# Memory heads over half jobs, late modulation panels outside the ring, half of the second layer's modulation sums in the first mixer

## The chip, the cores and the metric

One core of one Trainium2 chip runs the whole program. The metric is the device time of one execution in microseconds (us), as the median of several runs. Engine names: PE is the TensorE matmul, PEld its weight load, DVE VectorE, ACT ScalarE, POOL GpSimd, SP SyncE (here it only starts transfers).

## What is computed

Three blocks follow each other on 256 tokens of width 1024, all in float32. The first holds a mixer with three branches and a mixture of 16 experts; the second block has two layers, each with a mixer and a feed-forward part (dense in layer 0, eight experts in layer 1).

```python
# first block
proj = x @ w_in            # da_q da_k da_v r_q r_k r_v r_g m_q gates
y_da  = diff_attention(...)      # 8 heads
y_ret = silu(r_g) * retention(...)   # 4 heads
y_mem = memory_attention(m_q, mem @ w_mem_kv)   # 4 heads: softmax(q k) v
merged = sum_n sigmoid(gate_n) * (branch_n @ w_branch[n])
x = layer_norm(ALPHA * x + merged @ w_o); x = layer_norm(ALPHA * x + moe(x))
# second block
cond = silu(c)
for l in range(2):
    mod = cond @ ada_w[l] + ada_b[l]        # 6 vectors of 1024: shift, scale, gain
    h = x * (1 + sc_m) + sh_m; x = layer_norm(ALPHA * x + (1 + g_m) * mixer_l(h))
    h = x * (1 + sc_f) + sh_f; x = layer_norm(ALPHA * x + (1 + g_f) * ff_l(h))
```

## The kernel before, in words

**Precise products.** A float32 weight is used as two numbers: ACT writes a rounded copy ("hi"), DVE subtracts it from the weight and writes the rest ("lo"), and PE adds three products (hi with hi, hi with lo, lo with hi). In the mixers one such piece is 128x1024, called a chunk. A job (`gemm`) is two chunks of 24 matmuls of 256 columns; a "turned" job pair (`da_v`, `r_v`, `m_v`) is four chunks of 12 matmuls of 512 columns. hi copies stand in four places in turn (`HI_HOMES`), so ACT can't copy chunk n+4 before PE has used chunk n; the lo overwrites the panel in its slot.

**Order.** `mixer1_steps` writes the order of the first mixer out by hand. All engines walk the same list, each doing its part of a step, with semaphores between them. A `stage` step (hi and lo of a whole job) is put by `with_stages` ahead of the job before. In the eight first heads the steps are finer: `HEAD_FILL` gives each head two jobs, cut into four chunks (`part` for PE, `hi` for ACT, `lo` for DVE), laid between score, turn and out of the head. Two of the lo's (`now[2]`, `now[3]`) are made by DVE inside the two scores. The memory heads of the first mixer are coarser: a score, a whole `gate2` job, the turn of the head before, a whole `branch1` job, the out.

**Panels.** Weights come as panels of 2 MB, two jobs in each, on SP's queue, in the order of the plan. In the first mixer they go round four slots (`plan_loads`); a load waits until the panel that had the slot is done with, and SP stands still for it, so each later load waits as well.

**Modulation.** `mod` needs 24 panels of 2 MB of `ada_w_2` (12 per layer), each of which DVE multiplies with `cond_row` and sums, in four instructions (`sum_modulation`, L1408). Layer 0's twelve, steps `("ada", 0, n)`, go through the same four slots in the first mixer. Layer 1's twelve are taken in the dense feed-forward part: `half_loads` (L984) starts 24 loads of 1 MB from POOL into two places, and `sum_half` (L1418) makes one sum behind each of the 48 chunks 6 to 53 of 70. Load j may start when half j-2 has been summed.

**Feed-forward.** `unit` runs 70 chunks of the dense part: G, U (12 matmuls of 512 columns), turn, D. There are six places for chunks (`STAGES`) and three slots for panels. The lo of a chunk is L1764, the hi L1290; PE waits for the lo. SP starts the panel after next when DVE has made the four lo's of the slot's panel. For each pair DVE makes h (L1896) from ACT's silu (L1344), and PE may begin the next G only then where nothing else is in between.

**Table loads.** ACT's functions come in sets; `keep_ln_exp` loads the set with exp ahead of time. Sigmoid needs another set.

## Time and profile before

| | |
|---|---|
| median of 3 runs | 2211.27 us (2209.21 to 2212.22) |
| the profiled execution | 2206.13 us, its span 2204.3 us |
| first mixer, start to last of its matmuls | 0 to 485 us |
| dense feed-forward part | 886 to 1092 us |
| PE busy | 2101.5 us, 95% |
| DVE, ACT busy | 1750.0 us (79%), 1403.2 us (64%) |
| granted clock of TensorE, mean | 0.98 of full |

The profiled execution lies 5 us below the median, and its span 1.8 us below its own time. A row of the trace gives start, duration, engine, line, operation and, in square brackets, how long the engine stood idle before it and what ended that. A table of waits gives the sum, how many and the longest.

### The profile page before, as it was taken

To read this page: it belongs to the slowest core of one execution; us is meant where nothing else is said; L and a number is where in the kernel's file an instruction comes from. 1 tells how busy PE (TensorE), PEld (TensorE's weight loads), DVE (VectorE), ACT (ScalarE), POOL (GpSimd) and SP (SyncE) were. 2 spreads that over 40 slices of the span, in tenths; PEclk is the share of its full clock that TensorE was granted. 3 is DMA by queue.
4 is the path that set the end of the run, shared out by engine and by line. 5 is a ranking of instruction groups with operands and counts; after the bars stand their busy time and mean duration, and the time that the engine had idled before them with its cause. 6 is when DMAs were issued, how large, how long until landed. Compare 5 with 4: busy or idle time off the path is not lost.

```text
span 2204.3 us, 27381 instructions
## 1 busy us (share of the span) xinstructions
PE 2101.5 (95%) x10956; PEld 1788.4 (81%) x10956; DVE 1750.0 (79%) x2099; ACT 1403.2 (64%) x1707; POOL 42.7 (2%) x54
## 2 busy tenths in 40 slices
PE   8999999989999987899988999999999999999997
PEld 7888898888888876677878888888888888888886
DVE  2676677669988865767565899999999999999897
ACT  3566344547777654433353777887778778877774
POOL 0000000000000000000000000000000000000000
PEclk9999999989999999899998999999999999999999
DMA  8543676739999950678632799999999999999994
GB/s 313 210 153 115 252 300 254 282 125 376 385 372 375 376 196 1 256 297 311 235 160 115 287 392 368 389 365 390 361 388 362 393 377 375 379 367 378 386 395 152
DMA packets 59806, 659.26 MB, mean 299 GB/s; under 512 B 6288, under 2 KB 12304, under 8 KB 19088
## 3 DMA queue, kind: packets, MB, share of 16 engines
q1 hardware_dynamic: 49104, 608.32, 70.9%
q0 software_dynamic: 7152, 38.80, 4.4%
q10 hardware_dynamic: 3408, 10.22, 1.2%
q8 instruction: 92, 1.51, 0.3%
q14 instruction: 50, 0.41, 0.1%
HBM read 645.79 MB, written 11.53 MB: 298 GB/s over the span
## 4 chain that ended last, share of the span: by engine, by line
PE 77%; DVE 11%; DMA 7%; ACT 3%; issue 2%; ACTq 0%; DVEq 0%; SPq 0%
PE psum L2270 52%; PE psum L2012 11%; PE psum L1990 4%; DVE stage_lo L1764 3%; DMA arena<-ada_w_in 3%; PE psum L2059 3%; PE psum L1965 1%; PE psum L2405 1%; DMA ring<-moe_w_gate_in 1%; DVE arena L1418 1%; DVE ring L1408 1%; PE psum L2049 1%; DVE arena L767 1%; DMA ring<-moe_w_up_in 1%; DVE mixer_split L1532 1%
## 5 line engine op out<-in xcount | busy, mean ns | idle before, releaser
L1764 DVE TENSOR_TENSOR stage_lo<-ring,stage_hi 128x1024 fp32r<-128x1024 f32 (+1 forms) x934 | 1099.4, 1217 | 85.0 <-ACT stage_hi L1290 72.2
L1290 ACT ACTIVATE stage_hi<-ring 128x1024 fp32r<-128x1024 f32 (+1 forms) x934 | 953.4, 1053 | 281.3 <-PE psum L2270 151.8
L2270 PE MATMUL psum<-stage_hi,x_hi 128*128 128x512 f32 (+1 forms) x1344 | 531.6, 396 | 13.6 <-DVE arena L1896 10.1
L2270 PE MATMUL psum<-stage_hi,x_lo 128*128 128x512 f32 (+1 forms) x1344 | 522.2, 389 | 0.0
L2270 PE MATMUL psum<-stage_lo,x_hi 128*128 128x512 f32 (+1 forms) x1344 | 520.9, 388 | 0.0
L2270 PEld LDWEIGHTS psum<-stage_hi,x_hi 128*128 128x128 f32 x1344 | 253.4, 189 | 66.1 <-issue 10.3
L2270 PEld LDWEIGHTS psum<-stage_hi,x_lo 128*128 128x128 f32 x1344 | 252.9, 188 | 53.6
L2270 PEld LDWEIGHTS psum<-stage_lo,x_hi 128*128 128x128 f32 x1344 | 253.7, 189 | 49.0
L2270 PE MATMUL psum<-stage_hi,h_hi 128*128 128x512 f32 x664 | 261.9, 394 | 7.9 <-DVE stage_lo L1764 4.4
L2012 PE MATMUL psum<-mixer_split 128*128 128x256 f32 x1280 | 252.3, 286 | 13.4 <-DVE ring_split L1532 4.9
L2270 PE MATMUL psum<-stage_lo,h_hi 128*128 128x512 f32 x664 | 259.4, 391 | 0.0
L2012 PEld LDWEIGHTS psum<-mixer_split 128*128 128x128 f32 x1280 | 199.8, 193 | 16.7 <-issue 12.6
L2270 PE MATMUL psum<-stage_hi,h_lo 128*128 128x512 f32 x664 | 205.1, 390 | 0.0
L2012 PE MATMUL psum<-arena_split,mixer_split 128*128 128x256 f32 x928 | 187.8, 286 | 2.6 <-DVE mixer_split L1532 1.9
L1532 DVE TENSOR_TENSOR ring_split<-ring,mixer_split 128x1024 fp32r<-128x1024 f32 x98 | 116.2, 1220 | 63.0 <-ACT mixer_split L1042 62.9
L2270 PEld LDWEIGHTS psum<-stage_hi,h_hi 128*128 128x128 f32 x664 | 124.9, 188 | 36.0 <-DVE h_lo L1908 5.6
L2012 PEld LDWEIGHTS psum<-arena_split,mixer_split 128*128 128x128 f32 x928 | 145.4, 189 | 6.3 <-issue 5.8
L2270 PEld LDWEIGHTS psum<-stage_hi,h_lo 128*128 128x128 f32 x664 | 125.1, 188 | 26.5
L2270 PEld LDWEIGHTS psum<-stage_lo,h_hi 128*128 128x128 f32 x664 | 125.1, 188 | 25.1
L1042 ACT ACTIVATE mixer_split<-ring 128x1024 fp32r<-128x1024 f32 x98 | 99.3, 1053 | 46.3 <-DMA ring<-w_mem_kv_in 14.2
L1351 ACT ACTIVATE h_hi<-psum 128x512 fp32r<-128x512 f32 (+1 forms) x84 | 48.1, 580 | 84.4 <-PE psum L2405 84.4
L2012 PE MATMUL psum<-mixer_split,ring_split 128*128 128x256 f32 x304 | 85.4, 281 | 0.0
(266 smaller groups left out, 1971.6 us busy)
## 6 DMA issues: line engine op xcount, KB each, us to landing
ring<-moe_w_gate_in SPq DMA_DIRECT2D x56, 2048.0 KB, 9.7
ring<-moe_w_up_in SPq DMA_DIRECT2D x56, 2048.0 KB, 9.8
ring<-moe_w_down_in SPq DMA_DIRECT2D x56, 2048.0 KB, 10.0
ring<-w_in SPq DMA_DIRECT2D x48, 2048.0 KB, 10.1
ring<-w_in_in SPq DMA_DIRECT2D x12, 2048.0 KB, 8.6
arena<-ada_w_in POOLq DMA_DIRECT2D x24, 1024.0 KB, 7.7
ring<-ada_w_in SPq DMA_DIRECT2D x10, 2048.0 KB, 9.3
mixer_tiles<-w_in_in SPq DMA_DIRECT2D x7, 2048.0 KB, 8.5
```

The costliest lines, as they stand in the source:

```text
L767: settle(dve.bn_stats(bn_s[:, t, 6 * half:6 * half + 6], bank(b)))
L1042: act.activation(staged_hi(q, n), staged_source(q, c, False), ACT.Copy).then_inc(w_hi_set, 1)
L1290: act.activation(chunk_view(stage_hi, f, side, p, c), chunk_source(f, side, p, c), ACT.Copy)\
L1351: ins = act.activation(h_hi[:, 0:blocks, h_columns(f, p, t)], bank(t0 + t, 4, P)[:, 0:blocks, :], ACT.Copy)
L1408: ins = dve.tensor_tensor_reduce(wt[:, m, :], wt[:, m, :], cond_row, 1.0, 0.0, ALU.mult, ALU.add, mod[:, c:c + 1])
L1418: ins = dve.tensor_tensor_reduce(wt, wt, cond_row, 1.0, 0.0, ALU.mult, ALU.add, mod[:, c:c + 1])
L1532: dve.tensor_tensor(staged_source(q, c, True), staged_source(q, c, False), staged_hi(q, n).bitcast(F32), ALU.subtract).then_inc(w_lo_set, 1)
L1764: dve.tensor_tensor(chunk_view(stage_lo, f, side, p, c), chunk_source(f, side, p, c), chunk_view(stage_hi, f, side, p, c).bitcast(F32), AL ...
L1990: ins = pe.matmul(bank(banks[t]), xt[:, 2 * c + k, tokens], wt[:, k, :], start=(c + k + m == 0), stop=(c == 3 and k == 1 and m == 2))
L2012: ins = pe.matmul(bank(b, 2, T)[:, m, :], wt[:, k, :], xt[:, k, :], start=(k + j == 0), stop=(k == KT - 1 and j == 2))
L2059: ins = pe.matmul(bank(b, 2, T)[:, m, :], wt[:, k, c:c + P], rhs[:, k, :], start=(k == 0), stop=(k == KT - 1))
L2270: ins = pe.matmul(dst, a, b, start=start, stop=stop)
```

## The change

`ADA_MIXER1` = 18 panels are now summed in the first mixer: twelve of layer 0 and six of layer 1. Panels 0 to 10 go through the four slots. Panels 11 to 17 have a place of their own, `ada_late`, one panel in size, over the retention's q, k and v; POOL loads it (`late_loads`, ahead of its other work): the first when the last `ret_out` is done, each further one when the one before has been summed. Panels 3 to 6 are summed in halves, two instructions in each of the eight first heads; panels 0 to 2 lie between `da_k` and `da_v` jobs.

Each memory head now takes four chunks, `branch1` h and `gate2` h (`MEM_CHUNKS`), between score, turn and out, as the first heads do; the lo of `now[2]` is made inside the score. `keep_ln_exp` follows every sigmoid of gate 2 and the last of gate 1.

In the dense feed-forward part twelve loads of 1 MB and 24 sums stay; the first sum is at chunk 12, and then one at every second chunk.

```diff
@@ -49,6 +49,7 @@
...
 LAMBDA_INIT = 0.2
+ADA_MIXER1, ADA_LATE = 18, 11
...
@@ -121,6 +122,7 @@
...
+MEM_CHUNKS = [[((name, h), c) for name in ("branch1", "gate2") for c in range(2)] for h in range(MEM_H)]
...
@@ -173,8 +175,8 @@
...
-    s = gemms("da_q", 0) + splits("x", 0, 1, 2, 3) + gemms("da_q", 1, 2, 3) + gemms("da_k", 0, 1, 2, 3)
-    s += gemms("da_v", 0, 1) + ada(0) + [(side, *HEAD_CHUNKS[0][c]) for side in ("hi", "lo") for c in range(2)]
+    s = gemms("da_q", 0) + splits("x", 0, 1, 2, 3) + gemms("da_q", 1, 2, 3) + gemms("da_k", 0, 1) + ada(0)
+    s += gemms("da_k", 2, 3) + ada(1) + gemms("da_v", 0, 1) + ada(2) + [(side, *HEAD_CHUNKS[0][c]) for side in ("hi", "lo") for c in range(2)]
...
@@ -183,23 +185,26 @@
...
             s += [("da_norm", h - 1, 0)]
-        s += [("lo", *q) for q in nxt[:2]] + part(*now[2]) + [("hi", *q) for q in nxt[2:3]]
+        s += [("lo", *q) for q in nxt[:2]] + [("ada", 1 + h % 2, 3 + h // 2)] + part(*now[2]) + [("hi", *q) for q in nxt[2:3]]
...
         s += [("ret_out", h, 0)] + (splits("x_late", 0, 1, 2, 3) if h == RET_H - 1 else [])
-        s += [fill.pop(0)] + ada(1 + h) + [("ret_mean", h, 0)]
+        s += [fill.pop(0)] + ada(7 + h) + [("ret_mean", h, 0)]
         s += ([("ret_score", h + 1, 0)] if h + 1 < RET_H else []) + [fill.pop(0), ("ret_var", h, 0)]
-    s += gemms("gate1", 0, 1) + splits("mem", 0, 1, 2, 3) + gemms("gate1", 2, 3) + ada(5)
-    s += gemms("m_k", 0, 1) + ada(6) + gemms("m_k", 2, 3) + ada(7)
-    s += gemms("m_v", 0, 1) + ada(8) + gemms("m_v", 2, 3) + splits("yret", 0, 1, 2, 3) + ada(9)
-    s += [("mem_score", 0, 0)] + gemms("branch1", 0)
-    for h in range(1, MEM_H):
-        s += [("mem_score", h, 0)] + gemms("gate2", h - 1) + [("mem_turn", h - 1, 0)] + gemms("branch1", h)
-        s += [("mem_out", h - 1, 0)] + (ada(9 + h) if h < 3 else [])
-    s += splits("ymem", 0, 1, 2) + [("mem_turn", MEM_H - 1, 0)] + gemms("gate2", 3) + [("mem_out", MEM_H - 1, 0)]
-    s += splits("ymem", 3)
+    s += gemms("gate1", 0, 1) + splits("mem", 0, 1, 2, 3) + gemms("gate1", 2, 3) + ada(11)
+    s += gemms("m_k", 0, 1) + ada(12) + gemms("m_k", 2, 3) + ada(13)
+    s += gemms("m_v", 0, 1) + [(side, ("branch1", 0), c) for side in ("hi", "lo") for c in range(2)] + ada(14)
+    s += splits("yret", 0, 1) + gemms("m_v", 2, 3) + splits("yret", 2, 3) + [("hi", *MEM_CHUNKS[0][c]) for c in (2, 3)]
+    for h in range(MEM_H):
+        now = MEM_CHUNKS[h]
+        nxt = MEM_CHUNKS[h + 1] if h + 1 < MEM_H else [(("branch2", 0), 0), (("branch2", 0), 1)]
+        s += [("mem_score", h, 0), ("hi", *nxt[0]), ("lo", *now[3])] + part(*now[0]) + part(*now[1])
+        s += [("mem_turn", h, 0), ("hi", *nxt[1])] + (splits("ymem", 0, 1, 2) if h == MEM_H - 1 else [])
+        s += [("lo", *q) for q in nxt[:2]] + (ada(15 + h) if h + 1 < MEM_H else []) + part(*now[2])
+        s += [("hi", *q) for q in nxt[2:3]] + [("mem_out", h, 0)] + (splits("ymem", 3) if h == MEM_H - 1 else [])
+        s += part(*now[3]) + [("hi", *q) for q in nxt[3:]]
...
@@ -421,6 +426,7 @@
...
     cond_row = scratch(M_ADA, D)
+    ada_late = scratch(M_RQ, 4, D)
...
@@ -491,6 +497,7 @@
...
     ada_summed = sem("ada_summed")
+    ada_late_in = sem("ada_late_in")
...
@@ -675,7 +682,10 @@
...
                 free = (job_done, done[("ev_v", 0, 0)])
+            elif s[0] == "ada" and (s[1] == 2 or s[2] >= ADA_LATE):
+                continue
             elif s[0] == "ada":
+                key = ("ada", 0, s[2])
...
@@ -975,19 +985,29 @@
...
+        def late_loads():
...
+            pool.wait_ge(job_done, done[("ret_out", RET_H - 1, 0)])
+            for m in range(ADA_LATE, ADA_MIXER1):
+                if m > ADA_LATE:
+                    pool.wait_ge(ada_summed, m)
+                nc.gpsimd.dma_start(ada_late.rearrange("p a b -> p (a b)"), w["ada_w_2"][m // 12, m % 12]).then_inc(ada_late_in, 16)
...
             pool.wait_ge(job_done, done[("ln_back", 2, 3)])
-            for j in range(24):
+            for j in range(2 * (24 - ADA_MIXER1)):
...
                 nc.gpsimd.dma_start(ada_half[j % 2].rearrange("p a b -> p (a b)"),
-                                    w["ada_w_2"][1, j // 2][:, j % 2 * 2 * D:(j % 2 + 1) * 2 * D]).then_inc(ada_half_in[j % 2], 16)
+                                    w["ada_w_2"][1, ADA_MIXER1 - 12 + j // 2][:, j % 2 * 2 * D:(j % 2 + 1) * 2 * D]).then_inc(ada_half_in[j % 2], 16)
...
                 half_loads()
+            else:
+                late_loads()
...
@@ -1113,7 +1133,7 @@
...
                     ins.then_inc(bank_free[b], 1)
-                    if n == 2 and i == 3:
+                    if n == 2 or i == 3:
...
@@ -1370,7 +1390,7 @@
...
             act.wait_ge(job_done, plan_end[n])
-            act.wait_ge(ada_summed, 12)
+            act.wait_ge(ada_summed, ADA_MIXER1)
...
@@ -1397,29 +1417,34 @@
...
-        def sum_modulation(n):
+        def sum_modulation(n, part):
...
             layer, p = n // 12, n % 12
-            at, fill = panel[("ada", 0, n)]
-            dve.wait_ge(slot_full[at], 16 * fill)
-            wt = slot(at, 4)
-            for m in range(4):
+            if n < ADA_LATE:
+                at, fill = panel[("ada", 0, n)]
+                dve.wait_ge(slot_full[at], 16 * fill)
+                wt = slot(at, 4)
+            else:
+                dve.wait_ge(ada_late_in, 16 * (n - ADA_LATE + 1))
+                wt = ada_late
+            for m in ((0, 1, 2, 3), (0, 1), (2, 3))[part]:
...
                                                mod[:, c:c + 1])
-            ins.then_inc(ada_summed, 1)
+            if part != 1:
+                ins.then_inc(ada_summed, 1)
...
-            j, c = m // 2, 48 + m
+            j, c = m // 2, 4 * ADA_MIXER1 + m
...
                 ins.then_inc(ada_half_summed, 1)
-            if m == 47:
-                dve.wait_ge(ada_half_summed, 24)
+            if m == 4 * (24 - ADA_MIXER1) - 1:
+                dve.wait_ge(ada_half_summed, 2 * (24 - ADA_MIXER1))
...
@@ -1607,6 +1632,8 @@
...
                     dve.tensor_reduce(dmax, bank(b, 2, T), AX.X, ALU.max, negate=True).then_inc(mem_max, 1)
+                    job, c = MEM_CHUNKS[a][2]
+                    staged_low(("lo", *job), *staged_chunks(("lo", *job))[c])
...
@@ -1638,8 +1665,8 @@
...
                         dve.wait_ge(cond_set, 1)
-                    sum_modulation(i)
-                    if i == 11:
+                    sum_modulation(i, a)
+                    if i == 11 and a != 1:
...
@@ -1861,8 +1888,9 @@
...
                         take_tokens(fill, (n,))
-                    if not f["routed"] and 0 <= n - STAGES < 48:
-                        sum_half(n - STAGES)
+                    at = n - 2 * STAGES
+                    if not f["routed"] and at >= 0 and at % 2 == 0 and at // 2 < 4 * (24 - ADA_MIXER1):
+                        sum_half(at // 2)
...
```

## Rows read from the trace of the kernel before

**Rows 1.** Windows: stretch, length, busy PE, PEld, DVE, ACT, POOL, clock, DMA share, GB/s.

```profile
85.00:200.00 115.00, 114.11 (x814) 103.35 (x814) 81.68 (x122) 78.75 (x151) 0.00 (x0) 1.00 0.41 155
...
318.00:421.00 103.00, 93.83 (x628) 85.73 (x629) 70.93 (x99) 53.54 (x80) 0.00 (x0) 1.00 0.65 255
...
886.00:1092.00 206.00, 186.99 (x860) 153.85 (x860) 148.42 (x200) 80.36 (x94) 12.71 (x24) 0.96 0.75 290
```

**Rows 2.** Waits of PE in the dense feed-forward part, 886 to 1075 us.

```profile
PE psum L2270 <- DVE arena L1896: 10.1, 2, 8.5
PE psum L2270 <- DVE stage_lo L1764: 7.4, 6, 2.4
```

**Rows 3.** Waits of DVE in the same part, 886 to 1092 us.

```profile
DVE arena L1418 <- DMA arena<-ada_w_in: 32.3, 10, 4.4
```

**Rows 4.** Timeline of that part around PE's longest wait: ACT, DVE and PE rows.

```profile
909.22 1.02 ACT L1344 ACTIVATE arena<-psum 128x1024 f32<-128x1024 f32 x1 [0.30 <-PE psum L2270]
...
910.46 1.23 DVE L1418 CUSTOM_DVE_ANT_0 arena<-arena,mixer_tiles 128x1024 f32<-128x1024 f32 x1 [3.85 <-DMA arena<-ada_w_in]
...
916.18 1.28 DVE L1896 TENSOR_TENSOR arena<-arena,psum 128x512 f32<-128x512 f32 x2
...
917.72 0.77 PE L2270 MATMUL psum<-stage_hi,x_hi 128*128 128x512 f32 x1 [8.54 <-DVE arena L1896]
```

**Rows 5.** Waits of PE in the memory part of the first mixer, 317 to 422 us.

```profile
PE psum L2012 <- DVE ring_split L1532: 4.9, 4, 2.3
PE psum L1990 <- DVE ring_split L1532: 1.6, 1, 1.6
```

**Rows 6.** The sums of the dense feed-forward part, by line: busy, mean ns, idle before.

```profile
L1418 DVE CUSTOM_DVE_ANT_0 arena<-arena,mixer_tiles 128x1024 f32<-128x1024 f32 x48 | 58.6, 1221 | 32.3 <-DMA arena<-ada_w_in 32.3
```

**Rows 7.** Pieces of the chain that ended last, in the memory part: start, length, what.

```profile
318.19 5.86 PE psum L2012 x48
324.05 11.06 PE psum L1990 x48
...
371.91 1.73 PE psum L2141 x8
373.64 1.73 PE psum L2126 x8
```

**Rows 8.** Landing of a POOL load of 1 MB: started at 928.6 alone, at 962.2 in company.

```profile
DMA to landing us min/median/max: 5.2/5.2/5.2
...
DMA to landing us min/median/max: 9.7/9.7/9.7
```

**Rows 9.** Windows of 2 us after two of PE's waits, and one at full clock between.

```profile
918.00:920.00 2.00, 2.00 (x6) 1.54 (x6) 0.00 (x0) 0.00 (x0) 0.00 (x0) 0.50 0.96 410
...
924.00:926.00 2.00, 2.00 (x11) 1.63 (x9) 1.21 (x3) 2.00 (x4) 0.00 (x0) 1.00 0.00 0
...
1028.00:1030.00 2.00, 2.00 (x7) 1.52 (x6) 2.00 (x4) 0.00 (x0) 0.53 (x1) 0.50 0.92 254
```

**Rows 10.** Timeline of the memory part: the last of panel 5's four sums, and PE's job `m_k` 3.

```profile
302.31 1.22 DVE L1408 CUSTOM_DVE_ANT_0 ring<-ring,mixer_tiles 128x1024 f32<-128x1024 f32 x1
...
318.19 0.35 PE L2012 MATMUL psum<-mixer_split 128*128 128x256 f32 x1 [0.99 <-DVE ring_split L1532]
```

**Rows 11.** Landing of the 2 MB load that SP started alone at 99.2 us.

```profile
DMA to landing us min/median/max: 8.3/8.3/8.3
```

**Rows 12.** Timeline of heads 2 and 3 of the first eight: DVE, ACT and PE rows.

```profile
121.35 1.99 ACT L1042 ACTIVATE mixer_split<-ring 128x1024 fp32r<-128x1024 f32 x2
...
129.79 0.69 DVE L1565 SCALAR_TENSOR_TENSOR mixer_tiles<-arena,psum 128x512 f32<-128x512 f32 x1 [2.86 <-PE psum L2068]
...
136.93 0.69 DVE L1581 TENSOR_TENSOR mixer_tiles<-mixer_tiles 128x512 f32<-128x512 f32 x1
...
138.67 0.60 PE L1965 MATMUL psum<-arena,mixer_tiles 128*128 128x128 f32 x4
```

**Rows 13.** DMA issues of the page: median us to landing of three other POOL loads.

```profile
arena<-back POOLq DMA_DIRECT2D x3, 1024.0 KB, 16.2
```

## The prediction

> **What bounds the kernel now.** I read the windows by stage first. PE is busy nearly throughout the eight first heads, but for 187 of 206 us in the dense feed-forward part and for 94 of 103 in the memory part of the first mixer [rows 1]. The stages that the change doesn't touch move only as a whole. So the question is what PE waits for in these two, and whether what they lose is paid elsewhere.
>
> In the feed-forward part PE waits 17.5 us for DVE, 10.1 for h and 7.4 for lo's [rows 2]. DVE isn't short of time: it stands 32.3 us before the sums, waiting for the modulation loads [rows 3]. The timeline shows what is queued behind such a wait: silu is done at 910.24, but DVE waits 3.85 us for a half panel at 905 to 910, makes three lo's and three sums, and only then h at 916.18; PE stands for 8.54 us [rows 4]. In the memory part PE waits 9.9 us in ten pieces, mostly for lo's that are late since panels land late or sums of 4.6 us stand ahead of them; 6.5 of it are in [rows 5], and short ones for ACT's copies and for splits make up the rest.
>
> **The change part by part. 1: the feed-forward part.** A sum takes 1.22 us and the next instruction starts 1.14 after it [rows 6]. 24 of 48 go, and the rest come every second chunk. A chunk is 12 matmuls of 512 columns; 48 of these took 11.06 us in the mixer, 2.77 us each chunk [rows 7]. DVE then has two lo's and a sum, 3 x 1.14 = 3.4 us, per 5.5 of PE, where it had 4.6. What matters more is the time that a load gets. Load j starts when half j-2 is summed and is needed at the first sum of half j: three chunks later before, 8.3 us; six now, 16.6. It lands in 5.2 us alone and 9.7 beside a panel [rows 8]: too late for the old distance, in time for the new one in both cases. Halves 0 and 1 are there long before chunk 12. So all waits for these loads should go. Of the first wait a rest stays: silu ends at 910.24, h takes 1.28, and PE had stopped at 909.18, so about 2.6 us. Gain 17.5 - 2.6 = 14.9. The clock adds to it. It is at half (1.2 of 2.4 GHz) after the 8.54 us wait and again after the waits near 1027, with 6 or 7 matmuls in 2 us where 11 is normal [rows 9]. About 4.8 and 3.4 us run so, half of it lost: 4.1. If the 2.6 us that stay lower it again, 1 to 2 us of this are not won; I leave it at 4.1. Sum for this part -19.0; bounds -12 (a third of the waits stays) and -21.6 (none stays).
>
> **2: the memory heads.** They issue the same chunks, scores and turns; the finer order brings lo's forward and puts the turn behind a job of its own head, so its probabilities (some 3.5 us behind the score, an estimate from the timeline) are covered by the 5.86 us of a `branch1` job [rows 7]. With seven panels out of the ring, `m_v`, `gate2` and `branch` panels start 10 to 30 us earlier, so the waits for them go. Against that stands the new wait: DVE waits for `ada_late`, and its lo's are queued behind it. There is one place, so a load can't begin before the last sum. Panel 11 is summed by about 303.5, as panel 5 is now [rows 10]. Panel 12 starts then. On SP's queue 2 MB alone land in 8.3 us [rows 11]; for POOL's queue I take 1 MB alone, 5.2 [rows 8], and 2.6 for the second MB, at the 410 GB/s that a full window moves [rows 9]: 8 alone. In company, with the rest of `m_v` 2's panel in flight, I take 10.3: it lands at 313.8. Sums end at 318.4, the first lo of `m_k` 3 at 319.6. PE wants it at about 317.2, so it stands 2.4 us there, where it stands 0.99 now [rows 10]. The next two gaps are longer by the turned jobs (11.06 us [rows 7]) and fit. In a memory head PE needs about 15.7 us: four chunks of 2.93, score and out of 1.73 [rows 7], a turn of 0.6 [rows 12]. Load and sums need 10.3 + 4.6 = 14.9, so they fit by 0.8 us; DVE's own work there, sums included, is 12 us. I leave 1.0 us for pieces at the splits of `yret` and `ymem`. Waits 9.9 to 3.4: -6.5. Bounds -9 (loads land at once) and +3 (each load 2 us slower, which the three gaps between `m_k` and `m_v` and the heads pay). Table loads: the change moves each of them off the exp's front and adds one behind gate 1, on ACT, with DVE in sums meanwhile: nothing.
>
> The Trainium skill (DMA: Bandwidth & Descriptors, "Anatomy of one DMA") gives a load from this queue as about 2.0 us plus its bytes at 436 GB/s. That would be 4.4 us for 1 MB, where the row has 5.2, and 6.8 for 2 MB alone. By it load and sums would be 11.4 us and the stall at `m_k` 3 would go, 2.4 us better than my sum. The row decides, and the page says nothing here of company.
>
> **3: the first heads.** Sixteen sums come in, two a head, behind the lo's of `nxt` and ahead of the next score. DVE stands idle exactly there, for 2.86 us in head 3's case, and from 2.2 to 3.3 in the seven of this kind [rows 12]; 2 x 1.14 = 2.3 [rows 6] fit, and 0.5 is left of the cover. But a panel is released only by the second half, a head later. `r_v` 2's load is behind panel 3's second half: that ends at 115.9, and the load lands 8.3 us after its start [rows 11], at about 124.3, where ACT wants it at 121.35 [rows 12]. ACT's hi is 3.0 us late, DVE's norm and lo's behind it too; with the sums DVE reaches the next score 2.6 us late. PE's turn at 138.67 has 1.1 us of cover behind the probabilities, done at about 137.6 [rows 12], so it waits about 1.5 us. The same holds for `gate0` 2 behind panel 5. Sum +3.0, bounds 0 and +6. Before the heads `da_v` 2's panel now waits for `da_k` 3's slot (free at about 62.4) and lands 8.3 us later, 3 us before PE wants its lo, with hi and lo still to make: +0.3, up to +2. In the retention the sums and loads stand where they stood: 0.
>
> **Sum.** -19.0 - 6.5 + 3.0 + 0.3 = -22.2 us. Against the profiled span of 2204.3 that gives 2182; against the median 2211.3, which is how the result is measured, 2189. That execution was 5 us under the median; I take the difference over unchanged.
>
> **Rivals.**
> A (forecast), 2189, own range 2183 to 2196.
> B: the feed-forward gain comes, but the first mixer gets longer: 27 us more of DVE work in a stage where it is 71% busy in the heads [rows 1], with 0.5 us of cover a head. If each of the eight heads pays 0.5 to 1 us and the late loads take their upper bound, the mixer is +3 + 6 + 2: 2211 - 19 + 9 = 2201 with rounding down for what overlaps. For it: the cover is thin. Against: waits of the heads are independent, and a late DVE catches up in the first retention head.
> C: the gain in the feed-forward part is smaller, since another wait comes last there (lo's behind ACT, panels of SP behind POOL's): -8 instead of -19 and a mixer of about 0: 2203. Against: ACT is 39% busy there and DVE idles.
> D: slower. Place: the seven `ada_late` loads. Price: all DVE work is queued behind each. Three POOL loads of 1 MB landed in 16.2 us at the median [rows 13]; these have other rows and follow stores, but if a 2 MB load takes 16 us here, each of the six later panels is late: 16 + 4.6 = 20.6 against 11.4 (three gaps) and 15.7 (three), 42 us in all, 3 to 6 off for the lead. With -19 and +3 the result is 2211 - 19 + 3 + 38 = 2233. It decides from a landing of about 12 to 13 us on, where the stalls eat the 19 us. Against: the modulation loads of the same queue landed in under 10 us even in company [rows 8]. The Trainium skill (SBUF — State Buffer, "SBUF: two separate sides") has a rule that would bring this about: descriptors of a POOL transfer can't be written while DVE holds the port pair that both share. The trace doesn't bear it out for these instructions.
> E: the change does nothing that counts, since PE's waits have other causes: within 4 us of 2211. The timeline speaks against it.
>
> **How the numbers follow.** A 0.63, B 0.17, C 0.08, E 0.05, D 0.07. 0.2% is 4.4 us, about what a measurement of this kernel can tell from no change. A, and nearly all of B and C, are below 2206.8: faster 0.86. Same 0.07 (E and edges), slower 0.07 (D). The range takes A, B and part of C: 2181 to 2204.
>
> **What would show it.** After the change: PE's waits for L1896 in the feed-forward part at about 2.6 us, those for lo's near zero, DVE's wait for the half loads gone, and the part 19 us shorter; granted clock 1.00 there, but for its start. In the mixer a PE wait of 1 to 3 us before `m_k` 3, two waits of about 1.5 us at turns in heads 3 and 7, and PE's waits between 317 and 415 us at a third of now. The first mixer's last matmul moves from 484 to about 481. Wrong if DVE waits over 3 us before each `ada_late` sum of a head, if the heads grow by more than 6 us, or if PE's waits in the feed-forward part don't fall.

## The result and the profile after

| | before | after |
|---|---|---|
| median | 2210.53 us (2209.21 to 2212.22, 4 runs) | 2192.66 us (2189.59 to 2195.91, 4 runs) |
| the profiled execution | 2206.13 us, span 2204.3 us | 2189.59 us, span 2187.2 us |

The ratio of the times is 0.992, with an interval from 0.9906 to 0.9935: faster by 0.65 to 0.94%. The forecast of 2189.0 lies 3.7 us under the median, and the median is inside the forecast's range.

Events that both kernels have cut the two spans into six stretches: the start of the first retention score (end of the eight heads), the start of `gate1` 2 (a wait of 1.6 us), a wait of 0.75 us for a split of `merged` behind `branch2`, and the first and the last wait of the dense feed-forward part.

| stretch | before | after | difference | forecast |
|---|---|---|---|---|
| start to end of the eight heads | 200.43 | 210.40 | +9.97 | +3.3 |
| retention, to `gate1` 2 | 82.61 | 82.68 | +0.07 | 0 |
| memory part, to behind `branch2` | 161.25 | 153.73 | -7.52 | -6.5 |
| first norm and experts | 442.12 | 443.22 | +1.10 | 0 |
| dense feed-forward part | 206.13 | 184.85 | -21.28 | -19.0 |
| the rest | 1111.76 | 1112.32 | +0.56 | 0 |
| sum | 2204.3 | 2187.2 | -17.1 | -22.2 |

So the two gains came a little larger than forecast, and the heads cost three times what I had put down for them. Their +9.97 is even a little flattered: PE's first matmul came at 7.92 us instead of 9.05, since the first load of `x` landed earlier. From the first turn on the heads grew by 10.5 us.

**Dense feed-forward part.** PE's waits, from 890 to 1075 us, against [rows 2, 3],

```profile
PE psum L2298 <- DVE arena L1924: 2.6, 1, 2.6
PE psum L2298 <- DVE h_lo L1936: 1.5, 1, 1.5
PE psum L2298 <- DVE x_lo L1802: 0.5, 1, 0.5
PE psum L2298 <- DVE stage_lo L1791: 0.2, 1, 0.2
```

and DVE's:

```profile
DVE h_lo L1936 <- ACT h_hi L1371: 51.3, 6, 9.4
DVE stage_lo L1791 <- ACT stage_hi L1310: 9.3, 13, 1.6
```

DVE's wait for half panels is gone. It waits for ACT now, which costs PE nothing. The timeline at the place of [rows 4], DVE then PE:

```profile
911.69 1.22 DVE L1443 CUSTOM_DVE_ANT_0 arena<-arena,mixer_tiles 128x1024 f32<-128x1024 f32 x1
...
913.17 1.28 DVE L1924 TENSOR_TENSOR arena<-arena,psum 128x512 f32<-128x512 f32 x2 [0.26 <-ACT arena L1364]
...
914.72 0.47 PE L2298 MATMUL psum<-stage_hi,x_hi 128*128 128x512 f32 x1 [2.63 <-DVE arena L1924]
```

One sum stands before h, and h starts 0.26 us after DVE is free. PE's wait is 2.63 us, and the matmul after it runs at full clock (0.47 us, where the one behind the 8.54 us wait took 0.77). The whole part as a window (length, busy PE, PEld, DVE, ACT, POOL, clock, DMA share, GB/s):

```profile
890.03:1074.88 184.85, 180.45 (x860) 151.20 (x860) 121.89 (x153) 79.97 (x93) 6.24 (x12) 1.00 0.67 256
```

The full clock isn't a property of the change. The swap kernel below has the same part with the same wait, and there the clock is at half behind it:

```profile
907.50 0.76 PE L2305 MATMUL psum<-stage_hi,x_hi 128*128 128x512 f32 x1 [2.63 <-DVE arena L1931]
```

Of the 13 traces here that have this wait of 2.6 us, eight show 3.4 us at half clock around its end or up to 1.5 us behind it, which costs 1.4 to 1.6 us; in the other five (after, swap again, small sums, swap and early panel 11, sums at every chunk) the clock stays up. In all eight the first matmuls of the part ran at half clock too, in none of the five.

**The eight heads.** The window of the stretch after (length, busy PE, PEld, DVE, ACT, POOL, clock, DMA share, GB/s):

```profile
85.00:210.40 125.40, 117.82 (x813) 105.38 (x811) 99.81 (x154) 78.51 (x151) 0.00 (x0) 0.96 0.49 196
```

PE's waits in it:

```profile
PE psum L2110 <- ACT mixer_tiles L1048: 6.6, 2, 5.8
```

The timeline: ACT's hi of `r_g` 2, SP's start of panel 5 and, right behind it, of `r_g` 2 and `gate0` 0, and PE at the outs of heads 2 and 4:

```profile
158.84 2.00 ACT L1062 ACTIVATE mixer_split<-ring 128x1024 fp32r<-128x1024 f32 x2 [7.70 <-DMA ring<-w_in_in]
...
145.34 0.33 SPq L908 DMA_DIRECT2D ring<-ada_w_in  x1
145.71 0.91 SPq L908 DMA_DIRECT2D ring<-w_in_in  x2
...
128.13 1.13 PE L2110 MATMUL psum<-mixer_tiles,arena 128*128 128x256 f32 x4 [0.85 <-ACT mixer_tiles L1048]
163.13 2.07 PE L2110 MATMUL psum<-mixer_tiles,arena 128*128 128x256 f32 x4 [5.75 <-ACT mixer_tiles L1048]
```

PE stands 5.75 us before the out of head 4, whose copy ACT makes behind the hi of `r_g` 2; this hi had waited 7.70 us for its panel. The same four matmuls take 2.07 us there and 1.13 in head 2, so the clock fell to half behind the wait. Of the 10.0 us some 6 are waits and most of the rest is busy PE that runs slower: 117.8 us of busy time where the rows before had 114.1 [rows 1].

**The memory part.** PE's waits from 317 to 430 us, against [rows 5]:

```profile
PE psum L2040 <- DVE ring_split L1557: 2.3, 1, 2.3
PE psum L2040 <- DVE mixer_split L1571: 0.5, 1, 0.5
PE psum L2040 <- DVE mixer_split L1557: 0.3, 1, 0.3
```

The timeline of panel 12: POOL starts its load, DVE its first sum, and PE stands for `m_k` 3's lo behind the sums:

```profile
313.80 0.55 POOL L994 DMA_DIRECT2D mixer_tiles<-ada_w_in  x1 [43.46 <-DVE arena L1432]
...
323.54 1.23 DVE L1432 CUSTOM_DVE_ANT_0 mixer_tiles<-mixer_tiles 128x1024 f32<-128x1024 f32 x1 [3.63 <-DMA mixer_tiles<-ada_w_in]
...
329.50 0.36 PE L2040 MATMUL psum<-mixer_split 128*128 128x256 f32 x1 [2.30 <-DVE ring_split L1557]
```

The 0.5 us stand in the first memory head, ahead of its `branch1` chunk, and the 0.3 us behind the last head; otherwise PE doesn't wait in the four heads. The load of panel 12 landed after 9.7 us, and the wait in front of `m_k` 3 is 2.30 us, as worked out. Behind it the clock is at half for 3.4 us, which the forecast didn't count:

```profile
330.00:333.40 3.40, 3.40 (x18) 3.40 (x17) 2.75 (x3) 0.00 (x0) 0.00 (x0) 0.50 0.74 299
```

The second trace of the swap kernel has the same wait (2.52 us) without this, and its memory part takes 152.4 us instead of 153.7 to 153.9.

### The profile page after: what moved, and what is told of

Read it like the earlier page. It is cut to its first block, busy times and chain, and to the rows that moved or that the text cites. A ratio compares the mean times of both kernels' runs of the same rounds, so it can differ in the third digit from the quotient of the medians.

```text
span 2187.2 us, 27386 instructions
## 1 busy us (share of the span) xinstructions
PE 2101.9 (96%) x10956; PEld 1793.8 (82%) x10956; DVE 1750.7 (80%) x2099; ACT 1410.5 (64%) x1709; POOL 40.1 (2%) x49
## 4 chain that ended last, share of the span: by engine, by line
PE 87%; DVE 6%; DMA 3%; ACT 3%; issue 2%; DVEq 0%; ACTq 0%; SPq 0%
PE psum L2298 62%; PE psum L2040 11%; PE psum L2087 3%; PE psum L2018 2%; DMA ring<-w_in_in 2%; PE psum L2433 2%; PE psum L1993 1%; ACT mixer_split L1062 1%; DVE ring L1432 1%; PE psum L2077 1%; DVE mixer_tiles L1432 1%; PE psum L2308 1%; DVE mixer_split L1557 1%; DVE ring_split L1557 1%; PE psum L2197 0%
## 5 line engine op out<-in xcount | busy, mean ns | idle before, releaser
L2040 PE MATMUL psum<-mixer_split 128*128 128x256 f32 x1344 | 259.9, 289 | 10.6 <-DVE mixer_split L1571 4.7
L2040 PEld LDWEIGHTS psum<-mixer_split 128*128 128x128 f32 x1344 | 210.4, 196 | 13.3 <-issue 9.1
L1557 DVE TENSOR_TENSOR ring_split<-ring,mixer_split 128x1024 fp32r<-128x1024 f32 x106 | 125.7, 1219 | 55.2 <-ACT mixer_split L1062 55.1
L1062 ACT ACTIVATE mixer_split<-ring 128x1024 fp32r<-128x1024 f32 x106 | 108.3, 1054 | 61.1 <-PE psum L2040 26.2
L2040 PEld LDWEIGHTS psum<-arena_split,mixer_split 128*128 128x128 f32 x800 | 136.9, 190 | 5.6 <-issue 5.2
L2040 PE MATMUL psum<-arena_split,ring_split 128*128 128x256 f32 x352 | 99.5, 283 | 0.0
L1936 DVE TENSOR_TENSOR h_lo<-psum,h_hi 128x512 fp32r<-128x512 f32 (+1 forms) x84 | 56.5, 678 | 53.2 <-ACT h_hi L1371 52.6
```

The source lines that it names most:

```text
L1062: act.activation(staged_hi(q, n), staged_source(q, c, False), ACT.Copy).then_inc(w_hi_set, 1)
L1557: dve.tensor_tensor(staged_source(q, c, True), staged_source(q, c, False), staged_hi(q, n).bitcast(F32), ALU.subtract).then_inc(w_lo_set, 1)
L1936: ins = dve.tensor_tensor(h_lo[:, 0:blocks, part], bank(t0 + t, 4, P)[:, 0:blocks, :], h_hi[:, 0:blocks, part].bitcast(F32), ALU.subtract)
L2040: ins = pe.matmul(bank(b, 2, T)[:, m, :], wt[:, k, :], xt[:, k, :], start=(k + j == 0), stop=(k == KT - 1 and j == 2))
```

## The experiments

Times from the turn of head 0 to the end of the heads leave out the start of the program, which differs by up to 3 us between executions. "Memory part" and "feed-forward" are the stretches of the table above.

| kernel | heads from the first turn | memory part | feed-forward | time |
|---|---|---|---|---|
| before | 104.7 | 161.3 | 206.1 | 2206.1 |
| after | 115.2 | 153.7 | 184.9 | 2189.6 |
| swap | 107.1 | 153.9 | 186.6 | 2182.7 |
| swap, again | 106.8 | 152.4 | 184.9 | 2184.4 |
| small sums | 109.5 | 153.9 | 184.8 | 2189.7 |
| small sums and swap | 104.6 | 153.6 | 187.1 | 2181.2 |
| swap and exchanged slots | 105.0 | 154.1 | 187.1 | 2183.9 |
| these and early panel 11 | 105.2 | 156.8 | 187.2 | 2186.9 |
| all panels in the ring | 115.1 | 179.1 | 187.2 | 2219.8 |
| coarse heads, own place | 114.1 | 158.9 | 188.4 | 2201.4 |
| swap and early panel 11 | 106.7 | 156.4 | 184.8 | 2188.4 |
| swap and later panel 12 | 106.6 | 156.9 | 188.4 | 2190.5 |
| sums at every chunk | 115.2 | 153.9 | 191.1 | 2195.9 |
| feed-forward part alone | 104.6 | 159.4 | 186.6 | 2186.3 |

The time is that of the profiled execution in each row. "Small sums" (twice), "all panels in the ring", "coarse heads", "sums at every chunk" and "feed-forward part alone" were measured in this one execution only, so their stretches can be read, but their times only to a few us.

### Why the heads grew: the load behind another's wait, or DVE's work

```diff
+            order = list(loads[n])
+            if n == 0:
+                k = ring_keys.index(("ada", 0, 5))
+                order[k:k + 2] = order[k + 1], order[k]
```

> The changed kernel with two entries of SP's list of loads swapped: r_g 2's panel (slot 1, free since about 127.3 us) is started ahead of modulation panel 5 (slot 0, which waits for panel 4's second half, 145.3 us). Slots, sums and all work stay. Queue theory: the eight first heads grew by 10.0 us (end at 210.4 instead of 200.4) because r_g 2 stood behind that wait and landed at 158.8. Then it starts near 128, ACT's 7.7 us wait goes, PE's 5.75 us wait at the out of head 4 goes, and with it the 3 to 4 us at half clock behind it. First heads end at about 201.5 to 203, 7.5 to 9 us earlier, and the whole time is about 2184. Rival (more DVE work than the heads can cover): the sums are all still there, so the heads end within 2 us of 210.4 and the time stays at 2192.

Median 2182.54 us (2180.44 to 2193.41), ratio 0.9882 (0.9851 to 0.9913). All sums stay, and the stretch is 107.1 us instead of 115.2. SP's load of `r_g` 2 in the timeline:

```profile
126.16 0.33 SPq L911 DMA_DIRECT2D ring<-w_in_in  x1
```

What is left of ACT's waits for loads and of PE's waits, 95 to 201 us:

```profile
ACT mixer_split L1069 <- DMA ring<-w_in_in: 5.3, 3, 2.8
...
PE psum L2117 <- ACT mixer_tiles L1055: 1.3, 1, 1.3
```

The load starts at 126.2 instead of 145.7. The wait at head 4 and the slow matmuls behind it are gone. That settles the large part: one load's place in a queue cost 8 us.

```diff
+                k = 32 if part else D
-                ins = dve.tensor_tensor_reduce(wt[:, m, :], ...
+                ins = dve.tensor_tensor_reduce(wt[:, m, :k], ...
```

> The changed kernel with its 16 sums in the eight first heads over 32 columns instead of 1024: they leave out nearly all of the sum (so the modulation vectors of four panels are wrong), while the loads, their waits and the release of the slots stay. It takes away 16 x about 1.1 us of DVE work, 2.2 us a head. Queue theory: the wait of r_g 2's load stays, so PE's wait of 5 to 6 us at the out of head 4 stays and the heads end at 207 to 210 instead of 210.4; panel 4's second half is summed at most 2 us earlier. Rival (DVE work): the heads end at 200.4 to 202, as before the change.

The heads end at 203.9, between the two theories: 5.7 us less than after from the first turn. The wait is still there, but 3.02 us long, by the timeline of SP, ACT and PE:

```profile
140.04 0.33 SPq L908 DMA_DIRECT2D ring<-ada_w_in  x1
...
153.72 2.00 ACT L1062 ACTIVATE mixer_split<-ring 128x1024 fp32r<-128x1024 f32 x2 [5.22 <-DMA ring<-w_in_in]
...
158.02 1.13 PE L2111 MATMUL psum<-mixer_tiles,arena 128*128 128x256 f32 x4 [3.02 <-ACT mixer_tiles L1048]
```

Panel 4's second half ended 5.3 us earlier, not 2 (0.8 of it since PE's first turn came that much earlier), so both loads started 5.3 us earlier. Behind the wait of 3 us the first matmuls ran at full clock (1.13 us, not 2.07), and 1.2 us later it fell for 3.4 us:

```profile
159.20:162.60 3.40, 3.40 (x15) 2.62 (x16) 1.78 (x8) 3.36 (x5) 0.00 (x0) 0.50 1.01 410
```

Smaller sums thus shorten the wait through the queue as well, and the run alone can't tell the theories apart. The swap does.

What were the 2.4 us left with the swap? Two runs:

> The kernel with swapped loads and, beside that, the 16 sums in the eight first heads over 32 columns (they leave out nearly all of the sum, so four panels' modulation is wrong; loads and waits stay). From the turn of head 0 to the end of the heads the swap alone took 107.1 us, the kernel before 104.7. If the 2.4 us that stay are the loads (r_v 2 behind panel 3's second half, gate0 2 behind panel 5's), they shrink only as far as these second halves end earlier, to 1 to 2 us. If they are DVE work without cover, the stretch goes back to 104.7 within 0.3 us.

104.6 us: all of it went, which is what I had put down for DVE work as the cause. But again the loads moved too: ACT's wait for `r_v` 2 shrank from 2.82 to 0.99 us, and the one of 1.90 us for `gate0` 2 went. The other run keeps the sums and moves the load of `r_v` 2 alone:

```diff
+            crossed = crossed or key == ("gemm", "r_v", 2)
-            fill_slot(n, key, at % count, words, src, free)
+            fill_slot(n, key, 5 - at % count if crossed and not n and at % count > 1 else at % count, words, src, free)
```

> Both mends of the first heads together, without moving panel 11: r_g 2's load ahead of modulation panel 5's, and slots 2 and 3 exchanged from r_v 2 on, so that r_v 2 waits for r_k and no longer for panel 3's second half. All sums stay. Load theory (the 2.4 us by which the heads are longer than before with the swap alone are ACT's waits for r_v 2's load, not DVE work): from the turn of head 0 to the end of the heads 105.2 us, as in the kernel that had this exchange beside the early panel 11; PE's wait at m_k 3 stays at 2.4 us; the time is 1 to 2 us under the swap alone, 2181 to 2183. Rival (DVE work): the stretch stays at 107, and the time is that of the swap alone, 2183 to 2184.5.

The start of `r_v` 2's load in the timeline:

```profile
112.08 0.33 SPq L912 DMA_DIRECT2D mixer_tiles<-w_in_in  x1
```

ACT's waits for loads and PE's waits, 95 to 200 us:

```profile
ACT mixer_split L1070 <- DMA ring<-w_in_in: 2.4, 2, 1.8
...
PE psum L2001 <- issue: 0.4, 1, 0.4
```

105.0 us with all sixteen sums, 0.2 and 0.4 above the two traces with the old heads (104.7 and 104.6). So the sums themselves cost the heads at most 0.4 us, and DVE's cover of [rows 12] held. Median 2183.95 us (2183.36 to 2186.74), ratio 0.9887 (0.987 to 0.9904): the time is not the 1 to 2 us under the swap alone that I had expected. The 2 us gained in the heads can't be seen in the whole time beside the swap alone, whose second measurement is this:

> The kernel with swapped loads once more, unchanged, on the same chip as the one with panel 12 later, so that the two can be set side by side: about 2182.5 us as before, and 2 to 2.5 us more than with panel 12 later; if the stretches at half clock fall differently in the experts, the two differ by up to 3 us more or less than that.

Median 2184.35 us (2181.89 to 2189.18), ratio 0.9877 (0.9858 to 0.9897). The kernel with panel 12 later, which I had expected to be faster, was 4.4 us slower (below).

### What the memory part's gain is made of

```diff
-ADA_MIXER1, ADA_LATE = 18, 11
+ADA_MIXER1, ADA_LATE = 18, 18
```

> The changed kernel with all 18 panels of the first mixer in the four slots (no place of their own for the late ones, POOL loads none in the mixer). Own-place theory: most of the 7.5 us that the memory part gained comes from panels of m_v, gate2 and branch that no longer stand behind a modulation panel, so this part (m_k 0 to branch2 0, 127.4 us with the place, 134.9 before the change) gets 4 to 7 us longer, with DVE waits for loads ahead of sums and late lo's. Order theory (the finer order of the memory heads gives the gain): it stays within 2 us of 127.4. The first heads stay as in the changed kernel, about 210.

It was 25 us, far more than either theory had: 20.4 us more waits, and 5.0 us more busy time, with 11.9 us of it at half clock. PE stood at the turns of two heads and at one out. Its waits from 292 us on:

```profile
PE psum L1993 <- DVE mixer_tiles L1641: 14.5, 2, 8.9
PE psum L2169 <- ACT mixer_tiles L1048: 6.7, 1, 6.7
```

ACT's waits between 285 and 440 us say why:

```profile
ACT mixer_split L1062 <- DMA ring<-w_in_in: 21.4, 2, 14.2
ACT mixer_split L1062 <- DMA mixer_tiles<-w_branch_in: 13.2, 2, 10.3
```

The finer order takes `branch1` and `gate2` in turn and so holds two weight panels at once. With modulation panels between them in four slots, ACT waits 34.6 us for panels in the heads' hi's, and exp and the copies for out are queued behind them. In the changed kernel ACT has no such wait in this stretch. The other way round, the place without the order:

```diff
-        s += [("mem_score", h, 0), ("hi", *nxt[0]), ("lo", *now[3])] + part(*now[0]) + part(*now[1])
-        ...
+        s += [("mem_score", h, 0)] + gemms("gate2", h - 1) + [("mem_turn", h - 1, 0)] + gemms("branch1", h)
+        s += [("mem_out", h - 1, 0)] + ada(14 + h)
```

> The changed kernel with the coarse order of the memory heads of before, and the late panels still in their own place (panels 15, 16, 17 summed behind the outs of heads 0, 1, 2). Order theory: the finer order is what brings lo's forward; without it PE again waits for lo's in the heads, and the stretch from m_k 0 to branch2, 7.5 us shorter than before in the changed kernel, gives back 3 to 7 us. Place theory: the panels' own place gives the gain by itself, since the ring's loads then run 10 to 30 us ahead; then the stretch stays within 1.5 us of the changed kernel's, and the finer order is worth nothing here.

PE's waits in the stretch, 291 to 460 us:

```profile
PE psum L2035 <- DVE ring_split L1554: 4.7, 3, 2.3
PE psum L2035 <- DVE mixer_split L1554: 2.4, 1, 2.4
PE psum L2035 <- DVE mixer_split L1568: 1.7, 2, 0.9
PE psum L2164 <- ACT mixer_tiles L1045: 1.0, 2, 0.9
```

158.9 us: 5.2 of the 7.5 us are given back. So the place alone brings 2.3, both together 7.5, and the order alone costs 18 against the kernel before. The 2.3 are not certain: the run below with the feed-forward part alone has the old first mixer, unchanged, and took 159.4 us for this stretch, which leaves 0.5. The order can't be had without the place.

### The wait in front of `m_k` 3

Two attempts to remove its 2.3 us, both with the swap. Panel 11's sums before `gate1` 2:

```diff
-    ... splits("mem", 0, 1, 2, 3) + gemms("gate1", 2, 3) + ada(11)
+    ... splits("mem", 0, 1, 2, 3) + ada(11) + gemms("gate1", 2, 3)
```

> The changed kernel with the swapped loads (r_g 2 ahead of modulation panel 5) and, beside that, panel 11's sums moved ahead of gate1 2 instead of behind gate1 3. Panel 12's load can then start some 6 to 10 us earlier, its sums end before the lo of m_k 3 is due, and PE's wait of 2.3 us ahead of m_k 3 goes; 4.6 us of sums now stand ahead of the lo's of gate1 2 and 3, which have about 4 us of lead. Theory (the stall at m_k 3 is the late start of one load): 2 us less than with the swap alone, about 2180.5. Rival: the sums make a lo of gate1 late by 1 to 2 us, and the time is that of the swap alone, 2182.5.

PE's longest wait of the stretch in the timeline:

```profile
298.19 0.76 PE L2047 MATMUL psum<-arena_split,mixer_split 128*128 128x256 f32 x2 [4.66 <-DVE ring_split L1564]
```

The wait of 2.3 went and one of 4.66 us came, with the clock at half behind it (the pair of 0.76 us), and the memory part took 156.4 us instead of 153.9. Median 2187.87 us (2185.16 to 2193.69). The lead of 4 us that I had put down for these lo's isn't there: the sums' 4.6 us came out in full. The same with the exchanged slots beside it:

> The kernel with swapped loads and early panel 11, and beside that slots 2 and 3 exchanged from r_v 2 on. r_v 2's load then waits for r_k (slot 3, free when head 1 ends, about 112.5 us) instead of panel 3's second half (114.9 us), and gate0 2 and the panels behind keep their waits. Theory: r_v 2 lands about 2 us earlier, and PE's wait of 1.3 us at the out of head 2 goes; panel 6 now waits for r_v 2's slot-mate; in all 0.5 to 1.5 us less than without it. Rival: one of the later panels comes later by the exchange (modulation panel 7 or m_q 2 in the retention), and it costs 1 to 5 us.

Heads 105.2 instead of 106.7 us, as expected; the retention took 1.6 us longer. This is not the rival: PE's waits there are the same, but PE ran part of it at half clock, and the swap kernel did so too when it was measured again (below). Median 2186.17 us.

Panel 12's sums one job later:

```diff
-    s += gemms("m_k", 0, 1) + ada(12) + gemms("m_k", 2, 3) + ada(13)
+    s += gemms("m_k", 0, 1, 2) + ada(12) + gemms("m_k", 3) + ada(13)
```

> The kernel with swapped loads, and panel 12's sums one job later: between m_k 2 and m_k 3 in the order instead of ahead of m_k 2. DVE then makes the lo's of m_k 3 before it stands for panel 12. Theory: PE's wait of 2.4 us ahead of m_k 3 goes, since only DVE's place in its queue caused it and not the load itself; the sums of panel 12 run at about 313 to 317.5 and the first lo of m_v 0 is due at about 322, so nothing new waits. The stretch from gate1 2 to branch2 gets 2.4 us shorter, the time is about 2180. Rival: the lo's of m_v 0 and the load of panel 13, which both follow these sums, come late by 1 to 3 us, and the wait only moves there.

The timeline, DVE at panel 13 and PE behind it:

```profile
331.99 1.23 DVE L1439 CUSTOM_DVE_ANT_0 mixer_tiles<-mixer_tiles 128x1024 f32<-128x1024 f32 x1 [6.94 <-DMA mixer_tiles<-ada_w_in]
...
337.94 0.65 PE L2025 MATMUL psum<-mixer_split 128*128 128x512 f32 x1 [4.23 <-DVE ring_split L1564]
354.14 1.07 PE L2047 MATMUL psum<-mixer_split 128*128 128x256 f32 x7 [1.66 <-DVE mixer_split L1578]
```

The rival held, and larger: the sums ended 2.5 us later than with the swap alone (1.8 counted from `gate1` 2), panel 13's load started later by that and took longer (11.7 us instead of 10.1), DVE stood 6.94 us for it with the lo's of `m_v` queued behind. Median 2188.78 us (2184.36 to 2190.52), 4.4 us above the swap alone on the same chip. With one place for these panels, sums and load form a loop that is full; what one panel loses, the next pays.

### The feed-forward part by itself

```diff
-            for j in range(24):
+            for j in range(12):
...
-                    if not f["routed"] and 0 <= n - STAGES < 48:
-                        sum_half(n - STAGES)
+                    at = n - 2 * STAGES
+                    if not f["routed"] and at >= 0 and at % 2 == 0 and at // 2 < 24:
+                        sum_half(at // 2)
```

> The kernel before with one part of the change alone: in the dense feed-forward part twelve loads and 24 sums from chunk 12 on, one every second chunk. The first mixer is that of before, so six panels of the second layer are not summed at all and their columns are copied from the other six (this part of the modulation is wrong; the work of the last mixer and experts stays the same in kind). If the gain of this part is its own and owes nothing to the mixer, the part takes 184.9 us where its first matmul starts at full clock and about 186.6 where it starts at half, against 206.1 before; the first mixer stays at 484.0 us to its last matmul; the span is 2184 to 2186. If the mixer's new order helped the feed-forward part (other clock, other state of the queues), the part is longer than 188.

186.6 us, span 2184.2, both as expected. The gain is this part's own. The first mixer, which no edit touched, ended at 479.2 us, not at 484.0 as I had expected: the first matmul came 1.0 us earlier, the retention took 81.0 us without any half clock (82.6 before), and the memory part 159.4 with 9.1 us of waits (161.3 with 10.7). So what the mixer's side costs, sums and finer order together, is known only roughly. The table of stretches has 2.5 us, since the heads lost more than the memory part won; the spans have 3.0 (this run's is 20.1 us shorter than before, with the whole change 17.1); and counted to the end of the memory part the changed kernel is 7.3 us behind this run (446.8 against 439.5), 1.7 of it the clock in the retention.

Was it the time that a load gets, or half the work?

```diff
-                    if not f["routed"] and at >= 0 and at % 2 == 0 and at // 2 < 4 * (24 - ADA_MIXER1):
-                        sum_half(at // 2)
+                    if not f["routed"] and 0 <= at < 4 * (24 - ADA_MIXER1):
+                        sum_half(at)
```

> The changed kernel with the 24 sums of the dense feed-forward part at every chunk from the twelfth on, instead of every second: the same loads and sums, but a load has three chunks, 8.3 us, between its start and its use, as before the change, instead of six. Load-time theory: DVE again waits for half panels, up to 4 us for each that travels with a weight panel, some 10 to 16 us in all (half of the 32 before), and PE waits 4 to 9 us more for lo's and h than the 4.8 of the changed kernel; the part takes 190 to 196 us instead of 184.9. Work theory (the gain came from DVE having half the sums): the waits stay under 2 us and the part within 2 us of 184.9.

PE's waits in the part:

```profile
PE psum L2298 <- DVE arena L1924: 4.2, 2, 2.6
PE psum L2298 <- DVE stage_lo L1791: 3.6, 4, 2.2
```

and DVE's for loads:

```profile
DVE arena L1443 <- DMA arena<-ada_w_in: 17.7, 5, 4.4
```

The same 24 sums at the old distance bring back 17.7 us of DVE's waiting for loads, with the old longest wait of 4.4, and 6.3 us of the part (191.1). The spacing does what was said of it, and that is three tenths of the gain. The other seven tenths stay although the distance is the old one, so they come from what this run shares with the change: half as many sums and loads, and the first of them at chunk 12 instead of 6. No run separates these two.

The run also shows what a wait costs beside itself. Its window over the part:

```profile
889.61:1080.73 191.12, 181.70 (x861) 150.83 (x861) 121.95 (x153) 79.96 (x93) 6.24 (x12) 1.00 0.64 248
```

The clock is at 1.00 as in the changed kernel, but PE is busy for 181.7 us instead of 180.45, with four more waits. That is about 0.3 us of slower matmuls behind each wait, by this estimate.

## Why the prediction came out as it did

**Feed-forward part, right.** Its steps: all waits for half panels go (they did), the first wait keeps 2.6 us (2.63), lo waits near zero (0.2). Waits fell by 14.7 us, 14.9 forecast. The rest of the gain, which I had put down as 4.1 us of clock, is 6.5 us of busy time. The two stretches that I had named were sized right: 7.8 us busy at half clock, which cost 3.9. Two things were missing: the kernel before also started the part with 1.6 us at half clock (0.8), and six more waits at about 0.3 us each of slower matmuls, the estimate above, make 1.9. The risk that I had reckoned with, half clock behind the wait that stays, came in eight of the 13 traces and not in that of the changed kernel; why is open, and no edit of this part decides it. With the feed-forward part as in the changed kernel and half clock at the start and behind the wait, the part takes 186.6 to 188.4 us, a gain of 17.7 to 19.5. And "what matters more is the time that a load gets" was too strong: the distance by itself is worth 6.3 us.

**Memory part, right.** -7.5 against -6.5. The chain load 9.7 us (10.3 forecast), sums, lo's, PE's wait of 2.30 (2.4) came as worked out; at the splits and the last lo 0.9 us instead of 1.0. The waits fell by 6.8 us; the half clock behind the wait at `m_k` 3, about 1.5 us, wasn't in the sum, and fewer waits with their slow matmuls made up for it. Of the seven loads three let DVE wait, 3.63, 1.09 and 2.13 us, and only the first of these cost PE anything. The reason that I gave for the gain was incomplete: I took it for lo's brought forward and panels started earlier, as two effects that add up. The runs show a pair of which the order, alone, loses 18 us and the place, alone, gains little (0.5 to 2.3).

**The heads, wrong.** The failed step is "r_v 2's load is behind panel 3's second half ... The same holds for gate0 2 behind panel 5". I followed each weight panel to the panel that had its own slot. `r_g` 2's slot was free at 127, so I passed over it. But SP's queue is worked off in order, and between them stood panel 5's load, whose slot waits for panel 4's second half until 145.3. The brief note in my account of the kernel, that SP stands still for a waiting load and each later load waits as well, was the rule; the sum didn't use it for this one. The two cases that I did name were there and smaller: ACT waited 2.49 us for `r_v` 2 (3.0 forecast), which cost PE 0.85 us, at the out of head 2 and not at the turn of head 3, and 1.25 us for `gate0` 2, which cost nothing. With the swap, the kernel that has only the named waits, the stretch grew by 2.4 us against 3.0. Half clock behind a long wait wasn't in this term either: some 3 us of the ten. The term for `da_v` 2 was near: from the first matmul to the first turn it is 0.65 us more, with a wait of 0.72 us for a lo of `da_v`, against 0.3.

**The total.** One of the three signs of being wrong came: the heads grew by more than 6 us, beyond their upper bound. The first mixer's last matmul moved from 484.0 to 486.9 us, not to 481. That the time still lies 3.7 us from the forecast is in part luck: the 6.7 us missed in the heads were offset by 1.0 and 2.3 us more gain elsewhere, and 1.4 us or more of these hang on the clock behind one wait.

**Rivals.** B had the right place, a longer first mixer, but the wrong cause: work without cover costs at most 0.4 us in the heads. D didn't come, but it was nearer than the sum says. Six of the seven loads landed in 8.4 to 12.5 us, 9.7 for panel 12. The first one took longer than the 16 us that D had assumed:

```profile
DMA to landing us min/median/max: 17.7/17.7/17.7
```

It was started at 269.65 us beside two 2 MB loads of SP and one of ACT's, of which one of SP's took 20.6 us, with the DMA engines busy throughout (share 1.01 from 269.65 to 287.4 us). It cost nothing, since its first sum was due only at 308.8. The Trainium skill (SBUF — State Buffer, "SBUF: two separate sides") would have POOL's descriptors held up while DVE holds the shared ports, which it says of DVE's two-port mode. The six later loads show no such delay: SP's load that overlapped one of them landed in 9.9 us. Whether DVE used that mode here no trace tells. The long landing of the first doesn't need it, since SP's loads beside it were as late. C and E fell with the feed-forward part.

**The rest.** +1.7 us in stretches that the change doesn't touch. It is the clock, as below: PE is busy for about 3.7 us more in them and waits 1.7 us less.

## What to carry to other kernels

When a transfer is given a later release, list the queue that starts it and price every transfer behind it, also those whose own buffers are free: here one entry in the wrong place cost 8 us, more than all sixteen sums that the change had brought into the stage, and its exchange with the next gives the fastest kernel here that sums everything, 2182.5 us (ratio 0.9882; 2184.4 when measured again) against 2192.7. Background work on an engine that idles between due times can be free, but its loads need a distance of at least landing plus work: six chunks of 2.8 us did, three did not. A buffer with a single place makes load and use a closed loop, in which both attempts here moved the wait and didn't remove it; and a finer order that holds two panels at once may need a place of its own before it gains anything.

## What the runs showed that I had not expected

The same program runs the same stretch with nearly the same waits at different clocks. The swap kernel's retention in its first profile, a window with the columns as above:

```profile
204.70:237.50 32.80, 31.57 (x231) 30.04 (x231) 23.12 (x32) 13.66 (x21) 0.00 (x0) 1.00 0.52 212
```

and in its second:

```profile
203.80:238.20 34.40, 32.93 (x231) 31.39 (x231) 23.13 (x32) 13.65 (x20) 0.00 (x0) 0.95 0.53 208
```

231 matmul records in both, granted clock 1.00 and 0.95, and 1.6 us between them, 1.4 of it busy time. In the first norm and the experts, which no edit touched, the kernels took from 442.1 to 449.3 us; part of that is in the window around the norm, here of the changed kernel:

```profile
446.80:490.00 43.20, 38.35 (x274) 37.28 (x275) 25.48 (x73) 14.78 (x26) 0.00 (x0) 0.85 0.38 148
```

and of the swap kernel's second profile, over the same work:

```profile
435.30:478.50 43.20, 38.89 (x264) 37.90 (x264) 23.59 (x62) 13.16 (x23) 0.00 (x0) 0.80 0.35 135
```

274 matmul records in 43.2 us against 264. What decides whether the clock falls behind the same wait, and for how long, stays open; no run here separates it. So a gain of 2 us in one stage, such as that of the exchanged slots, shows in the stage's own stretch and not in the median.

A POOL load of 1 MB in the feed-forward part landed in 5.6 us at the median, 5.1 at least and 12.5 at most, where [rows 8] had 5.2 and 9.7 and all 24 before had a median of 7.7; the six chunks' distance covered even the longest.
